# Expert weights mapped to partitions in contiguous runs: a two-block transformer kernel with two mixture-of-experts layers

## Chip, cores, metric

The kernel runs on one core of one Trainium2 chip, in one launch. The metric is the device time in microseconds. Everything is float32.

## What is computed

The reference runs 512 tokens of width 1024 through a first block (an even layer with pooling and differential attention, an odd layer with latent attention and a gated delta rule, each with a gated embedding layer behind it) and then, with 16 meta tokens put in front, through a second block of two layers: forgetting attention and a gated recurrence, each followed by a mixture of experts. The change touches the two mixtures alone:

```python
def hier_moe(h, w_grp, b_grp, w_rt, b_rt, w_up, w_down):     # h is already normalised
    # pick the best of 4 groups of experts, then the best 2 of its 8 experts
    ...
    def expert_block(args):
        xb, e = args                                        # 64 rows of tokens, one expert
        gate_up = xb @ w_up[e]                              # 1024 x 1024
        a, u = jnp.split(gate_up, 2, axis=-1)
        return (jax.nn.silu(a) * u) @ w_down[e]             # 512 x 1024
    ...
```

There are 32 experts a layer, so a layer reads 32 up matrices of 4096 KB and 32 down matrices of 2048 KB.

## The kernel before

The program is a list of stages, each a block in which the five engines run their own instruction lists; the next stage starts when all of them are through with the block. SBUF holds a ring of four weight buffers of 16 KB a partition, the transposed hidden rows `hT` (8 x 528 floats a partition), the rows themselves, and an arena that the stages share.

A mixture layer (`moe_layer`) has five stages. `stage_norm` squares and scales the rows, transposes them on TensorE (L365) and multiplies by the layer's gain on the way out of PSUM (VectorE, L343). In the same block SyncE issues what its argument `ahead` names: four small loads of the router (L2113 to L2116) and the weights of the first two experts (`first_pair`: up, down, up, down). `stage_route` waits for the router's loads (`loaded.at(64)`), computes logits with TensorE (L373, products of 36 columns) and picks experts in a long chain of VectorE steps. `stage_dispatch` scatters the rows of `keep`, which are normalised but not yet multiplied by the gain, into `x_rows` in HBM, 64 slots an expert. `stage_experts` is the loop. `stage_combine` gathers the results and adds them to the hidden rows.

`stage_experts` runs 16 times over a pair of experts. The up weights have two buffers, one over two ring buffers (`weight_ring` in the profile) and one in the arena; the down weights have the other two ring buffers. So each expert of a pair has its own buffers, and a buffer is loaded again as soon as the product that reads it is done (SyncE waits in the order up 0, down 0, up 1, down 1). In an iteration:

- SyncE loads 128 rows, those of both experts (L2364); TensorE transposes them in eight instructions (L2368), VectorE places them in `xT` with the gain (L2374).
- `tensor_up` (L2381): per expert 8 slices of the contraction times 2 halves of the columns, 512 columns each. The row block of 64 is the stationary operand, the weights are the moving one. The two halves q go to PSUM partitions 0 to 63 and 64 to 127. The profile shows each product as two instructions, 32 an expert.
- ScalarE takes silu of the first half (L2437), VectorE multiplies (L2455), TensorE transposes the hidden block (L2386), ScalarE places it (L2439).
- `tensor_down` (L2393): 16 instructions an expert. VectorE copies the result (L2459), ScalarE's queue stores it.

A weight matrix is mapped as `(k p)`: partition p holds the rows p, 128 + p, 256 + p and so on, each a run of 4 KB in HBM. Because the up products' columns are split in the order `(s q c)` (s: gate or value, q: half, c: 256 columns), a product reads runs of 256 neighbouring floats.

Of the kernel before, what the change touches and what calls it, by code (L numbers as in the profile page):

```python
# [13 lines left out]
P = 128  # L14
D = 1024
KD = D // P
# [21 lines left out]
ROWS = 64  # L38
# [37 lines left out]
class Signal:  # L76


    def __init__(self, sem):
        self.sem, self.base, self.count = sem, 0, 0  # L80
# [289 lines left out]
def products(nc, out, left, right):  # L370

    for i, (l, r) in enumerate(zip(left, right)):
        last = nc.tensor.matmul(out, l, r, start=i == 0, stop=i == len(left) - 1)  # L373
    return last
# [310 lines left out]
class Pooling:  # L685
# [11 lines left out]
    def load(self, sp):  # L697
        a = self.g.a
        sp.dma_start(self.scale, a["ev_pool_scale"].rearrange("a (n p) -> p (a n)", p=P), allow_slow_non_contiguous=True).then_inc(*self.loaded.up(16))
        sp.wait_ge(*self.zeroed.at(1))  # L700
        for n in range(2):
            for m in range(2):
                sp.dma_start(self.wp[64 * m:64 * m + 64, n, 64 * m:64 * m + 64], a["ev_pool_w"][2 * n + m]).then_inc(*self.loaded.up(16))
# [1375 lines left out]
class ExpertWeights:  # L2079
# [7 lines left out]
        self.wu, self.wd = g.a["moe_w_up_2"][layer], g.a["moe_w_down_2"][layer]  # L2087

    def load_up(self, sp, e, n):
        return sp.dma_start(self.up[n], self.wu[bass.ds(e, 1)].rearrange("a (k p) f -> p (a k) f", p=P))  # L2090

    def load_down(self, sp, e, n):
        return sp.dma_start(self.down[n], self.wd[bass.ds(e, 1)].rearrange("a (k p) f -> p (a k) f", p=P))

    def first_pair(self, sp):

# [5 lines left out]
class Router:  # L2102


    def __init__(self, g, layer):
        self.layer, self.a = layer, g.a
        self.w = g.take(KD, GROUPS + NEXP)
        self.bias = g.take(GROUPS + NEXP)
        self.loaded = g.sig("router_loaded")

    def load(self, sp):
        w, bias, a, n = self.w, self.bias, self.a, self.layer
        sp.dma_start(w[:, :, 0:GROUPS], a["moe_w_grp_2"][n].rearrange("(k p) n -> p k n", p=P), allow_slow_non_contiguous=True).then_inc(*self.loaded.up(16))  # L2113
        sp.dma_start(w[:, :, GROUPS:], a["moe_w_rt_2"][n].rearrange("(k p) n -> p k n", p=P)).then_inc(*self.loaded.up(16))
        sp.dma_start(bias[:, 0:GROUPS], a["moe_b_grp_2"][n:n + 1].to_broadcast([P, GROUPS])).then_inc(*self.loaded.up(16))
        sp.dma_start(bias[:, GROUPS:], a["moe_b_rt_2"][n:n + 1].to_broadcast([P, NEXP])).then_inc(*self.loaded.up(16))  # L2116


def moe_layer(g, layer, ring_upto):
    g.top = 0  # L2120
    keep = g.take(5, D)

    gw = g.take(2, 5)
    dest = g.take(2, 5).bitcast(I32)
    over = g.take(OVER + 1).bitcast(I32)
    g.top += (-g.top) % 8
    weights = ExpertWeights(g, layer)
    router = Router(g, layer)

    def ahead(sp):  # L2130
        router.load(sp)
        weights.first_pair(sp)

    tiles = XT if layer else ALLT
    stage_norm(g, tiles, g.gain(4 + layer), g.fed, keep, ahead)
    stage_route(g, tiles, router, gw, dest, over)
    stage_dispatch(g, tiles, keep, dest)
    stage_experts(g, layer, over, weights)
    g.top = 5 * D + 64
    stage_combine(g, tiles, gw, dest, ring_upto)  # L2140
    g.top = 0


def stage_route(g, tiles, router, gw, dest, over):

    nc = g.nc
    mark = g.top
    loaded = router.loaded
# [23 lines left out]
    with nc.Block() as block:  # L2172
        @block.tensor
        def _(pe):
            pe.wait_ge(*loaded.at(64))
            for i, t in enumerate(tiles):
                a, n = TILES[t]
                last = products(nc, g.psum[0:n, i, 0:NL], [g.hT[:, k, a:a + n] for k in range(KD)], [w[:, k, :] for k in range(KD)])
                last.then_inc(*ready.up())

            pe.wait_ge(*counted.at(1))
            for i, t in enumerate(tiles):
                n = TILES[t][1]
                left = [one[0:TILES[k][1], 0:n] for k in tiles if k < t] + [g.c("before")[0:n, 0:n]]
                products(nc, g.psum[0:n, 5, i * NEXP:(i + 1) * NEXP], left, [both[0:TILES[k][1], k, :] for k in tiles if k <= t])
            products(nc, g.psum[:, 6, 0:NEXP], [one[0:TILES[k][1], :] for k in tiles], [both[0:TILES[k][1], k, :] for k in tiles]).then_inc(*counts_ready.up())
# [9 lines left out]
        def _(dve):  # L2196
# [20 lines left out]
            dve.wait_ge(*chain.last())  # L2217
            v.memset(C, 0.0).then_inc(*chain.up())
            dve.wait_ge(*chain.last())
            dve.wait_ge(*loaded.at(64))  # L2220
            for i, t in enumerate(tiles):
                n = TILES[t][1]
                dve.wait_ge(*ready.at(i + 1))
# [50 lines left out]
            for i, t in enumerate(tiles):  # L2274
                n = TILES[t][1]
# [66 lines left out]
def stage_experts(g, layer, over, weights):  # L2342


    nc = g.nc
# [2 lines left out]
             "gated", "gate_silu", "hidden_transposed", "hidden_placed", "down_ready", "result_placed", "result_free_0", "result_free_1"]  # L2348
    x_in, x_turned, x_placed, up_ready, hid, silu, h_turned, h_placed, dn_ready, y_placed, y_free0, y_free1 = g.sig(*names)
    up_in, dn_in, y_free = weights.up_in, weights.down_in, (y_free0, y_free1)  # L2350
    gain = g.gain(4 + layer)
    up, down = weights.up, weights.down

    x = g.hT[:, 0:2, 0:512]
    xT = g.hT[:, 2:4, 0:512].rearrange("p a (k r) -> p a k r", k=4)
    s = g.hT[:, 6, 0:256]
    act_ = g.hT[:, 6, 256:512]
# [2 lines left out]
    xr, yr = g.a["x_rows"], g.a["y_rows"]  # L2360
    PAIRS = NEXP // 2

    def load_rows(sp, blk, rows):
        return sp.dma_start(x[0:rows, :, :], xr[bass.ds(blk * ROWS, rows)].rearrange("r (a c) -> r a c", a=2))  # L2364

    def tensor_rows():
        for c in range(KD):
            last = nc.tensor.transpose(g.psum[:, c // 4, (c % 4) * P:(c % 4 + 1) * P], x[:, c // 4, (c % 4) * P:(c % 4 + 1) * P], g.c("identity"))  # L2368
        return last

    def place_rows():
# [3 lines left out]
        return last  # L2375

    def tensor_up(n):
        wv = up[n].rearrange("p k (s q c) -> p k q s c", s=2, q=2)
        for k in range(KD):
            for q in range(2):  # L2380
                last = nc.tensor.matmul(g.psum[64 * q:64 * q + 64, 2 + n, :].rearrange("p (s c) -> p s c", s=2), xT[:, k // 4, k % 4, ROWS * n:ROWS * n + ROWS], wv[:, k, q, :, :], start=k == 0, stop=k == KD - 1)  # L2381
        return last

    def tensor_hidden():
# [17 lines left out]
    with nc.Block() as block:  # L2402
        @block.sync
        def _(sp):
            load_rows(sp, 0, P).then_inc(x_in.sem, 16)
            with sp.Fori(1, PAIRS) as i:
                sp.wait_ge(x_turned.sem, i + x_turned.base)
                load_rows(sp, 2 * i, P).then_inc(x_in.sem, 16)
                for n in range(2):

                    sp.wait_ge(up_ready.sem, 2 * i + (up_ready.base + n - 1))
                    weights.load_up(sp, 2 * i + n, n).then_inc(up_in[n].sem, 16)

                    sp.wait_ge(dn_ready.sem, 2 * i + (dn_ready.base + n - 1))
                    weights.load_down(sp, 2 * i + n, n).then_inc(dn_in[n].sem, 16)

        @block.tensor
        def _(pe):
            with pe.Fori(0, PAIRS) as i:
                pe.wait_ge(x_in.sem, 16 * i + (x_in.base + 16))  # L2420
                tensor_rows().then_inc(x_turned.sem, 1)
                pe.wait_ge(x_placed.sem, i + (x_placed.base + 1))
                for n in range(2):
                    pe.wait_ge(up_in[n].sem, 16 * i + (up_in[n].base + 16))
                    tensor_up(n).then_inc(up_ready.sem, 1)
                    pe.wait_ge(hid.sem, 2 * i + (hid.base + n + 1))
                    tensor_hidden().then_inc(h_turned.sem, 1)
                    pe.wait_ge(h_placed.sem, 2 * i + (h_placed.base + n + 1))
                    pe.wait_ge(dn_in[n].sem, 16 * i + (dn_in[n].base + 16))
                    tensor_down(n).then_inc(dn_ready.sem, 1)  # L2430
# [41 lines left out]
    with nc.Block() as block:  # L2472
# [8 lines left out]
        @block.sync  # L2481
        def _(sp):
            def body(j):
                e = sp.value_load(over[0:1, bass.ds(j, 1)], min_val=0, max_val=NEXP - 1)
                sp.wait_ge(done, j + 1)
                load_rows(sp, j + NEXP, ROWS).then_inc(rows_l, 16)
                weights.load_up(sp, e, 0).then_inc(up_l, 16)
                weights.load_down(sp, e, 0).then_inc(down_l, 16)
            each(sp, body)

        @block.tensor
        def _(pe):
            def body(j):
                pe.wait_ge(rows_l, 16 * j + 16)
                tensor_rows().then_inc(rT, 1)
                pe.wait_ge(rp, j + 1)
                pe.wait_ge(up_l, 16 * j + 16)
                tensor_up(0).then_inc(ur, 1)
                pe.wait_ge(ga, j + 1)
                tensor_hidden().then_inc(hT_, 1)  # L2500
                pe.wait_ge(hp, j + 1)
                pe.wait_ge(down_l, 16 * j + 16)
                tensor_down(0).then_inc(dr, 1)
            each(pe, body)
# [641 lines left out]
```

## Time and profile before

| | us |
|---|---|
| median of three runs | 3334.73 |
| lowest, highest | 3331.75, 3338.49 |
| the profiled execution: time | 3341.96 |
| the profiled execution: span | 3340.1 |
| PE busy, share of the span | 80% |
| DVE, ACT, POOL busy | 26%, 15%, 13% |
| mean granted TensorE clock | 0.874 |

Durations come from the profiled execution. Engines are PE (TensorE), PEld (its weight loads), DVE (VectorE), ACT (ScalarE), POOL (GpSimd) and SP (SyncE); SPq is SyncE's queue of issues. A row of a window has the window and its length, the busy time and number of instructions of PE, PEld, DVE, ACT and POOL, then the granted clock as a share of full speed, the mean busy share of the 16 DMA engines, and GB/s. `out<-in` names tensors of the program.

### The profile page before, as it was taken

The numbers are of one execution on the slowest core, as the hardware profiler recorded it, in microseconds if no ns is written. First come the engines' busy times: TensorE is split into PE (matmuls) and PEld (weight loads), VectorE is DVE, ScalarE is ACT, GpSimd is POOL, SyncE is SP. The second block draws the span as 40 slices with busy tenths as digits, with TensorE's granted clock in tenths as the row PEclk, the third lists the DMA queues.
The fourth block names the chain that finished last, engine by engine and source line by source line (L and its number), as shares of the span: only waits on it lengthen the run. The fifth ranks groups of instructions, "written<-read, shape, count | busy, mean of one in ns | idle before, by whom it ended". The sixth has DMA issues, their size and how long they took to land. (4 is left out here: it accounts for less than half of the span.)

```text
span 3340.1 us, 31732 instructions
## 1 busy us (share of the span) xinstructions
PE 2668.4 (80%) x12346; PEld 1339.6 (40%) x12346; DVE 871.8 (26%) x1847; ACT 498.9 (15%) x1154; POOL 448.6 (13%) x681
## 2 busy tenths in 40 slices
PE   6988888995757898999838777775989875777774
PEld 3654444452556544456432222222435442222221
DVE  2315411124366213205131110103055422101111
ACT  1102101012300002115100000001134300000000
POOL 1510001006010002217110000002044200000001
PEclk9995599997778999989959999997989887998987
DMA  4220012102000004203349999995101035999997
GB/s 148 76 91 1 0 54 76 51 16 91 1 1 1 26 8 147 76 8 120 143 195 367 416 415 417 415 416 172 36 27 52 26 153 220 415 417 415 416 415 289
DMA packets 196225, 570.13 MB, mean 171 GB/s; under 512 B 21040, under 2 KB 31152, under 8 KB 195984
## 3 DMA queue, kind: packets, MB, share of 16 engines
q1 hardware_dynamic: 181136, 534.77, 41.0%
q0 software_dynamic: 4736, 17.04, 1.4%
q10 hardware_dynamic: 10240, 16.79, 1.4%
q8 instruction: 74, 1.21, 0.1%
q14 instruction: 39, 0.32, 0.0%
HBM read 524.23 MB, written 44.21 MB: 170 GB/s over the span
## 5 line engine op out<-in xcount | busy, mean ns | idle before, releaser
L373 PE MATMUL psum<-weight_ring,hidden_T 128*128 128x512 f32 (+3 forms) x1792 | 714.1, 557 | 14.5 <-DMA arena<-in_p_T 10.4
L373 PEld LDWEIGHTS psum<-weight_ring,hidden_T 128*128 128x128 f32 x1792 | 339.0, 194 | 364.8 <-issue 290.6
L2381 PE MATMUL psum<-weight_ring,hidden_T 128*64 128x512 f32 x1024 | 284.0, 717 | 102.8 <-DMA weight_ring<-in_moe_w_up 95.9
L2393 PE MATMUL psum<-weight_ring,hidden_T 128*64 128x512 f32 x1024 | 233.8, 599 | 30.3 <-ACT hidden_T L2439 30.3
L2381 PE MATMUL psum<-arena,hidden_T 128*64 128x512 f32 x1024 | 230.0, 602 | 27.1 <-DMA arena<-in_moe_w_up 27.0
L2381 PEld LDWEIGHTS psum<-weight_ring,hidden_T 128*64 128x64 f32 x1024 | 94.5, 164 | 272.0 <-issue 257.1
L2455 DVE TENSOR_TENSOR hidden_T<-hidden_T,psum 128x256 f32<-128x256 f32 x64 | 27.0, 422 | 603.4 <-ACT hidden_T L2437 603.4
L2563 POOL DMA_INDIRECT arena<-expert_rows_out,arena x18 | 21.3, 1185 | 1067.8 <-PEq L2552 1062.9
L275 POOL TENSOR_SCALAR arena<-arena 128x1 f32<-128x1 f32 (+5 forms) x97 | 20.9, 215 | 941.5 <-ACT arena L1091 186.6
L2381 PEld LDWEIGHTS psum<-arena,hidden_T 128*64 128x64 f32 x1024 | 71.8, 138 | 184.6 <-issue 132.8
L2393 PEld LDWEIGHTS psum<-weight_ring,hidden_T 128*64 128x64 f32 x1024 | 67.8, 136 | 155.1 <-issue 109.6
L2437 ACT ACTIVATE hidden_T<-psum 128x256 f32<-128x256 f32 x64 | 24.5, 383 | 692.9 <-PE psum L2381 692.9
L2685 PE MATMUL psum<-weight_ring,hidden_T 128*128 128x512 f32 x256 | 123.4, 612 | 0.0
L2459 DVE COPY arena<-psum 128x512 f32<-128x512 f32 x64 | 44.3, 692 | 301.7 <-PE psum L2393 301.7
L373 PE MATMUL psum<-hidden_T,weight_ring 128*128 128x512 f32 (+2 forms) x288 | 119.4, 576 | 3.5 <-PEq L298 3.5
L373 PE MATMUL psum<-weight_ring,arena 128*128 128x512 f32 (+1 forms) x240 | 115.8, 629 | 2.1 <-PEq L2662 1.0
L2677 PE MATMUL psum<-hidden_T,weight_ring 128*128 128x512 f32 x256 | 111.4, 595 | 3.8 <-PEq L298 1.8
L365 PE MATMUL psum<-constants,arena 128*128 128x128 f32 (+1 forms) x216 | 40.2, 363 | 82.2 <-ACT arena L325 80.7
L279 POOL TENSOR_TENSOR arena<-arena,constants 128x1 f32<-128x1 f32 (+5 forms) x89 | 94.9, 1066 | 7.4
L2368 PE MATMUL psum<-constants,hidden_T 128*128 128x128 f32 x256 | 36.7, 289 | 65.0 <-DMA hidden_T<-expert_rows_in 65.0
L373 PE MATMUL psum<-arena,hidden_T 128*128 128x36 f32 (+2 forms) x264 | 61.8, 413 | 30.9 <-PEq L298 18.3
L457 DVE TENSOR_TENSOR hidden<-hidden,psum 128x512 f32<-128x512 f32 (+1 forms) x34 | 23.4, 687 | 221.4 <-PE psum L373 220.8
(461 smaller groups left out, 3169.9 us busy)
## 6 DMA issues: line engine op xcount, KB each, us to landing
weight_ring<-in_moe_w_up SPq DMA_DIRECT2D x32, 4096.0 KB, 23.3
weight_ring<-in_moe_w_down SPq DMA_DIRECT2D x64, 2048.0 KB, 24.0
arena<-in_moe_w_up SPq DMA_DIRECT2D x32, 4096.0 KB, 25.5
hidden_T<-expert_rows_in SPq DMA_DIRECT2D x32, 512.0 KB, 19.9
expert_rows_out<-arena ACTq DMA_DIRECT2D x128, 128.0 KB, 5.5
weight_ring<-in_hg_w_in SPq DMA_DIRECT2D x8, 2048.0 KB, 8.8
weight_ring<-in_ev_w_in SPq DMA_DIRECT2D x8, 1536.0 KB, 6.7
weight_ring<-in_fox_w_in SPq DMA_DIRECT2D x6, 2048.0 KB, 8.5
```

Source lines behind the costliest of these rows:

```text
L279: g.nc.gpsimd.tensor_tensor(out, out, power, ALU.pow).then_inc(*done.up())
L365: last = nc.tensor.transpose(g.psum[:, 2 * (i % 2) + c // 4, (c % 4) * P:(c % 4) * P + n], src, g.c("identity")[0:n, 0:n])
L373: last = nc.tensor.matmul(out, l, r, start=i == 0, stop=i == len(left) - 1)
L457: nc.vector.tensor_tensor(dst, dst, g.psum[0:n, u % 4, :], ALU.add).then_inc(*added.up())
L2368: last = nc.tensor.transpose(g.psum[:, c // 4, (c % 4) * P:(c % 4 + 1) * P], x[:, c // 4, (c % 4) * P:(c % 4 + 1) * P], g.c("identity"))
L2381: last = nc.tensor.matmul(g.psum[64 * q:64 * q + 64, 2 + n, :].rearrange("p (s c) -> p s c", s=2), xT[:, k // 4, k % 4, ROWS * n:ROWS * n ...
L2393: last = nc.tensor.matmul(g.psum[64 * q:64 * q + 64, 6 + n, :], aT[:, k % 2, 64 * (k // 2):64 * (k // 2) + 64], down[n][:, k, 512 * q:512 ...
L2437: nc.scalar.activation(s, g.psum[:, 2 + n, 0:256], ACT.Silu).then_inc(silu.sem, 1)
L2455: nc.vector.tensor_tensor(act_, s, g.psum[:, 2 + n, 256:512], ALU.mult).then_inc(hid.sem, 1)
L2459: nc.vector.tensor_copy(y[n], g.psum[:, 6 + n, :]).then_inc(y_placed.sem, 1)
L2677: last = mm(bank(u % 2), w[:, k, (x % 4) * P:(x % 4 + 1) * P], g.hT[:, k, META:], **flags)
L2685: last = mm(bank(u % 2), g.hT[:, k, a:a + n], w[:, k, :], **flags)
```

## The change

The weights are mapped as `(p k)`: partition p holds eight neighbouring rows of the up matrix, 8p to 8p + 7, and four neighbouring rows of the down matrix, 4p to 4p + 3. Slice k of the contraction is then every eighth channel, so the row transposes take every eighth element of a row (`x[:, c::KD]`), and the gain that is multiplied in behind them must be laid out likewise. That layout, `row_gain`, comes from eight more small loads in the router's list (each 16 partitions of 8 single floats), and the router's waits count them (192 instead of 64). The rows of tokens now lie in one run of 1024 floats instead of two of 512. Hidden channel 4p + k must stand in slice k of the down product, so the up product takes its columns at a step of four: `(s c q j)` instead of `(s q c)`.

```diff
     def load_up(self, sp, e, n):
-        return sp.dma_start(self.up[n], self.wu[bass.ds(e, 1)].rearrange("a (k p) f -> p (a k) f", p=P))
+        return sp.dma_start(self.up[n], self.wu[bass.ds(e, 1)].rearrange("a (p k) f -> p (a k) f", p=P))
     def load_down(self, sp, e, n):
-        return sp.dma_start(self.down[n], self.wd[bass.ds(e, 1)].rearrange("a (k p) f -> p (a k) f", p=P))
+        return sp.dma_start(self.down[n], self.wd[bass.ds(e, 1)].rearrange("a (p k) f -> p (a k) f", p=P))
...
+        g.row_gain = g.take(KD)
...
+        by_chunk = a["norm_gains"].rearrange("(r k) (n q) -> n q r k", k=KD, q=KD)
+        for q in range(KD):
+            sp.dma_start(self.g.row_gain[16 * q:16 * q + 16, :], by_chunk[4 + n, q], allow_slow_non_contiguous=True).then_inc(*self.loaded.up(16))
...
-            pe.wait_ge(*loaded.at(64))
+            pe.wait_ge(*loaded.at(192))
...
-            dve.wait_ge(*loaded.at(64))
+            dve.wait_ge(*loaded.at(192))
...
-    gain = g.gain(4 + layer)
+    gain = g.row_gain
...
-    x = g.hT[:, 0:2, 0:512]
+    x = g.hT.rearrange("p k n -> p (k n)")[:, 0:D]
...
-        return sp.dma_start(x[0:rows, :, :], xr[bass.ds(blk * ROWS, rows)].rearrange("r (a c) -> r a c", a=2))
+        return sp.dma_start(x[0:rows, :], xr[bass.ds(blk * ROWS, rows)])
...
-            last = nc.tensor.transpose(g.psum[:, c // 4, (c % 4) * P:(c % 4 + 1) * P], x[:, c // 4, (c % 4) * P:(c % 4 + 1) * P], g.c("identity"))
+            last = nc.tensor.transpose(g.psum[:, c // 4, (c % 4) * P:(c % 4 + 1) * P], x[:, c::KD], g.c("identity"))
...
-        wv = up[n].rearrange("p k (s q c) -> p k q s c", s=2, q=2)
+        wv = up[n].rearrange("p k (s c q j) -> p k q s j c", s=2, q=2, j=2)
         for k in range(KD):
             for q in range(2):
-                last = nc.tensor.matmul(g.psum[64 * q:64 * q + 64, 2 + n, :].rearrange("p (s c) -> p s c", s=2), xT[:, k // 4, k % 4, ROWS * n:ROWS * n + ROWS], wv[:, k, q, :, :], start=k == 0, stop=k == KD - 1)
+                last = nc.tensor.matmul(g.psum[64 * q:64 * q + 64, 2 + n, :].rearrange("p (s j c) -> p s j c", s=2, j=2), xT[:, k // 4, k % 4, ROWS * n:ROWS * n + ROWS], wv[:, k, q, :, :, :], start=k == 0, stop=k == KD - 1)
```

## Rows read from the trace of the kernel before

**Rows 1.** The page's slices: GB/s of the DMA engines in 40 slices.
```profile
GB/s 148 76 91 1 0 54 76 51 16 91 1 1 1 26 8 147 76 8 120 143 195 367 416 415 417 415 416 172 36 27 52 26 153 220 415 417 415 416 415 289
```
**Rows 2.** Window over the first expert stage; the DMA queues in 1850 to 2200 us.
```profile
1748.26:2262.60 514.34, 404.86 (x1728) 137.63 (x1728) 55.56 (x95) 43.77 (x79) 0.00 (x0) 0.93 0.99 398
...
DMA packets 39795, 145.50 MB, mean 416 GB/s; under 512 B 1522, under 2 KB 1522, under 8 KB 39795
```
**Rows 3.** The page's groups of the up product: busy, mean ns, idle before.
```profile
L2381 PE MATMUL psum<-weight_ring,hidden_T 128*64 128x512 f32 x1024 | 284.0, 717 | 102.8 <-DMA weight_ring<-in_moe_w_up 95.9
L2381 PE MATMUL psum<-arena,hidden_T 128*64 128x512 f32 x1024 | 230.0, 602 | 27.1 <-DMA arena<-in_moe_w_up 27.0
```
**Rows 4.** Timeline of TensorE, second expert pair: start us, us, what.
```profile
1778.78 1.10 PE L2368 MATMUL psum<-constants,hidden_T 128*128 128x128 f32 x8
1781.26 7.09 PE L2381 MATMUL psum<-weight_ring,hidden_T 128*64 128x512 f32 x32 [1.38 <-DVE hidden_T L2374]
...
1793.67 7.04 PE L2381 MATMUL psum<-arena,hidden_T 128*64 128x512 f32 x32
...
1806.15 1.09 PE L2368 MATMUL psum<-constants,hidden_T 128*128 128x128 f32 x8
```
**Rows 5.** Timeline: first transposes and last copy of each expert stage.
```profile
1748.26 1.97 PE L2368 MATMUL psum<-constants,hidden_T 128*128 128x128 f32 x8 [33.63 <-DMA hidden_T<-expert_rows_in]
...
2262.66 0.69 DVE L2459 COPY arena<-psum 128x512 f32<-128x512 f32 x1 [4.67 <-PE psum L2393]
...
2791.68 1.97 PE L2368 MATMUL psum<-constants,hidden_T 128*128 128x128 f32 x8 [31.41 <-DMA hidden_T<-expert_rows_in]
...
3307.16 0.69 DVE L2459 COPY arena<-psum 128x512 f32<-128x512 f32 x1 [4.67 <-PE psum L2393]
```
**Rows 6.** VectorE groups by form: reductions, contiguous (L2298, L910), strided (L2238, L2976).
```profile
L2298 DVE TENSOR_REDUCE arena<-arena 128x5 f32<-128x160 f32 x6 | 1.9, 321 | 0.2
L2238 DVE TENSOR_REDUCE arena<-arena 128x40 f32<-128x160 f32 x1 | 0.4, 420 | 0.0
...
L910 DVE TENSOR_REDUCE arena<-arena 128x6 f32<-128x768 f32 x4 | 3.8, 953 | 0.1
...
L2976 DVE TENSOR_REDUCE weight_ring<-weight_ring 128x128 f32<-128x768 f32 x8 | 12.1, 1510 | 0.3
```
**Rows 7.** TensorE groups by form: four 32-column products side by side.
```profile
L389 PE MATMUL psum<-weight_ring,arena 128*32 128x128 f32 x512 | 16.2, 274 | 1.6 <-POOL arena L439 1.6
```
**Rows 8.** Timeline from the norm to the router, both layers; windows (columns of rows 2).
```profile
1664.71 15.58 SPq L2093 DMA_DIRECT2D weight_ring<-in_moe_w_down  x1
...
1671.12 2.48 DVE L343 TENSOR_TENSOR hidden_T<-psum,norm_gains 128x512 f32<-128x512 f32 x4 [0.36 <-PE psum L365]
1680.73 11.51 PE L373 MATMUL psum<-arena,hidden_T 128*16 128x36 f32 x64 [8.76 <-PEq L298]
...
2731.02 13.84 PE L373 MATMUL psum<-arena,hidden_T 128*128 128x36 f32 x64 [9.56 <-PEq L298]
...
1690.00:1695.00 5.00, 5.00 (x25) 5.00 (x25) 0.20 (x1) 0.00 (x0) 0.00 (x0) 0.50 1.03 423
...
1700.00:1705.00 5.00, 0.13 (x2) 0.12 (x2) 4.28 (x24) 0.21 (x1) 0.00 (x0) 0.50 0.00 0
```
**Rows 9.** Packets and issues of the page; issue and landing of two small loads.
```profile
DMA packets 196225, 570.13 MB, mean 171 GB/s; under 512 B 21040, under 2 KB 31152, under 8 KB 195984
...
q8 instruction: 74, 1.21, 0.1%
q14 instruction: 39, 0.32, 0.0%
...
1.23 0.49 SPq L212 DMA_DIRECT2D constants<-in_constants  x1
...
constants<-in_constants SPq DMA_DIRECT2D x1, 1664.5 KB, 6.8
...
arena<-in_moe_w_grp SPq DMA_DIRECT2D x2, 16.0 KB, 2.3
```

More of the change, by code:

```diff
@@ L2105, in __init__ @@
     def __init__(self, g, layer):
-        self.layer, self.a = layer, g.a
+        self.g, self.layer, self.a = g, layer, g.a
         self.w = g.take(KD, GROUPS + NEXP)
         self.bias = g.take(GROUPS + NEXP)
+        g.row_gain = g.take(KD)
         self.loaded = g.sig("router_loaded")
```

## The prediction

> **What bounds the kernel now.** I read the page first, by its slices of DMA throughput [rows 1]. Twice it stands at 413 to 418 GB/s for many slices in a row: these are the two expert stages, the only place where the changed loads run. The window over the first of them [rows 2] says the same in one number each: 514 us, DMA share 0.99, TensorE busy 405 us. In the steady part the queues move 416 GB/s with 4 KB packets, and the packets' own time fills the 16 engines. The groups of the up product [rows 3] show whom TensorE waits for there: of the idle time before them, 95.9 and 27.0 us end with the landing of an up matrix. So the transfers bound these stages. How near TensorE is behind them is to be read where they do not yet bind: the first expert pairs of a stage find their weights loaded. The second pair of the first stage [rows 4] runs from its row transposes at 1778.78 to the next pair's at 1806.15: 27.37 us, with no wait for a transfer. The stage from its first transpose to its last copy [rows 5] takes 2263.35 - 1748.26 = 515.1 us, and 516.2 us in the second layer: some 32.2 us a pair. TensorE and its chain have 4.8 us of slack in a pair, no more. 14.1 us of the 27.37 are the up products, 7.09 and 7.04 us an expert.
>
> **Part 1, the up product's reads.** Its instructions keep count and shape (32 an expert, 512 columns), but the moving operand now takes every fourth float32 of the weight row, so neighbours stand 16 bytes apart instead of 4. Each now lasts some 600 ns [rows 3], yet 32 of them take 7.04 us [rows 4]: they run two at a time, one for each half of the up columns, and a pair follows the last after (7.04 - 0.60) / 15 = 430 ns, 0.84 ns a column for each of the two streams. No row shows TensorE reading at a stride. The nearest rows are VectorE's [rows 6]. A reduction of 160 contiguous elements takes 321 ns, one of 768 takes 953: 1.04 ns an element and 155 ns fixed. The same 160 elements read 32 bytes apart take 420 ns, so (420 - 155) / 160 = 1.66 ns an element; 768 read 512 bytes apart take 1510 ns, 1.76 ns an element. An SBUF read in which each element stands apart from the last costs 1.66 to 1.76 ns on that engine, and TensorE asks for one every 0.84 ns. Lower end: nothing, if TensorE's port brings separate elements at that pace. For that speaks [rows 7]: four 32-column products side by side read four streams of float32, 512 instructions in 16.2 us, 126 ns for four times 128 columns, so the engine is fed by more than one stream at near full pace; but all of them contiguous. Upper end: 1.76 ns an element, or, if both streams of a pair share it, 3.3 to 3.5. I take 1.66 ns a column with the streams independent, since the stride of 32 bytes is the nearest one measured and [rows 7] shows that streams do not add up. A pair of instructions then takes 512 x 1.66 = 850 ns instead of 430: 420 ns more, 16 times an expert, 6.7 us an expert, 13.4 us an expert pair.
>
> Weighed against the notes: the Trainium skill, "Advanced Engine Details and Errata", section "SBUF Cachelines", says that reads want at least two hits in a 16-byte line, and that a new line for each access is penalised. With float32 sixteen bytes apart there is one hit. VectorE's two strided rows agree (1.66 and 1.76 ns against 1.04); no row here tries it on TensorE. The page gives no factor; by it the sum is that of my forecast in kind, and without it that of the first rival.
>
> **Part 2, the row transposes.** Eight an expert pair; the stationary operand takes every eighth float32 of the row. They take 1.10 us now, 137 ns each. At 1.66 ns an element a load of 128 takes 212 ns: 75 ns more, 0.6 us a pair. Lower end nothing. They lie on TensorE's chain.
>
> **Part 3, does it show?** The 4.8 us of slack a pair are used up when the up products grow by more than a third. With 13.4 + 0.6 us more they are, and then the chain runs at its own pace. That pace for a whole stage: first pair 30.52 us (1748.26 to 1778.78, with a slow clock at its start), 15 more at 27.37: 441 us. Add 16 x 14.0 = 224: 665 us. Against 515.1 and 516.2 us that is 150 and 149 more, together +299 us. The granted clock is 0.93 over the stages now; with no transfer to wait for it stays up, as in the pair of [rows 4], which is the one that I count with. Nothing takes the extra time back: the next layer needs the sums of all experts.
>
> **Part 4, the transfers.** Each partition of an up matrix now reads one run of 32 KB instead of eight rows of 4 KB, a down matrix 16 KB instead of four; the rows of tokens go as 4 KB instead of twice 2 KB. Bytes are the same. That a run goes as one packet can be counted [rows 9]: of 196225 packets 195984 are under 8 KB, so 241 are above; 74 + 39 are instruction fetches, and the 128 left are the 128 partitions of the constants (1664.5 KB, 13 KB each). Throughput can hardly rise, the engines being filled: between 416 GB/s as now and 423, the best 5 us with 4 KB packets [rows 8], 1.7%, up to 8.5 us a stage. In my forecast the transfers no longer bind, so it counts nothing. By the Trainium skill, "DMA: Bandwidth & Descriptors", section "Why small descriptors are slow (HBM only)", each packet has some 3 bus cycles of its own, 2.3% of one of 4 KB; that estimate would give 11 us a stage in place of 8.5 and leaves the forecast as it is.
>
> **Part 5, SyncE's queue before the router.** This gives something back. SyncE issues the first pair's four loads in the norm block, and its last issue takes 15.58 us, to 1680.29, since descriptors back up [rows 8]. The norm's last VectorE step is done at 1673.60, yet the router's products start at 1680.73, 0.44 us after SyncE: TensorE idles 8.76 us there, 9.56 us in the second layer. With 128 runs a load instead of 1024 and 512 the issues should take what the constants took, about 0.5 us each. The eight new gain loads (128 runs of 4 bytes each) stand ahead of them: 8 x 0.49 = 3.9 us of issue, and the wait counts them too. The router's group weights, 1024 short runs, land in 2.3 us [rows 9], so the gains are there by about 1669, SyncE is through by 1668.2, and the router starts at 1673.60 + 0.44: 6.7 us earlier, and 0.8 more in the second layer, where the idle time is that much longer: -14.2 us in all. The first pair's own landing moves 3.9 us later, to about 1700 (DMA is idle from 1700 now), while the first token rows are transposed at 1748 [rows 5]: hidden. If the issues still back up, the 3.9 us come on top in each layer: +7.8. The row gain takes eight columns of the arena; the multiplication by it is as before. VectorE and ScalarE have the same work.
>
> **Sum.** +299 - 14 = +285 us on the profiled execution's own time of 3341.96 (span 3340.1): 3627. The median of the runs, 3334.73, is 7.2 us lower than that execution; so 3620 us.
>
> **Rivals.** (Each as a median, 7.2 us below the sum.)
> (a) TensorE reads at this stride at full pace, or less than a third slower: the slack hides it. Then the transfers still bind, and what is left is part 5 and up to 17 us of part 4: 3341.96 - 14.2 - 8.5 - 7.2 = 3312 (3303 to 3320): faster. For it speak [rows 7] and that the port is another than VectorE's. Against it VectorE's rows. It decides at 27.37 + 4.8 us a pair: a pitch of 430 + 4800 / 32 = 580 ns a pair of instructions.
> (b) As (a), but the issues still back up: +7.8 us, less what throughput gives: 3326 to 3342, about no change.
> (c) The stride costs a factor and not a time: 1.66 / 1.04 = 1.6 times. 686 ns a pair, 8.2 us an expert pair more, 441 + 131 = 572 us a stage: +114 - 14 = +100: 3435.
> (d) Both streams share the line rate: pitch 1700 ns, 40.6 us an expert pair more: 441 + 650 = 1091 us a stage, about 4470.
> (e) Long runs slow the transfers, since each engine then stays long in one place of the memory and stores wait behind long packets. No row speaks for it; the constants' 13 KB packets ran at the common rate. At 5% it is +50 us: 3370 with the rest of (a).
>
> **How the numbers follow.** Forecast (with its upper end of 1.76 ns, no part 2 at the lower) 0.50; (c) and what lies between 0.07; (d) 0.03; (e) 0.02; (a) 0.31; (b) 0.07. The likeliest case's own range: 3600 (part 2 free) to 3700: 512 x 1.76 = 901 ns, 15.1 us a pair, 441 + 242 + 10 = 693 us a stage, +355, and +7.8 if issues back up, less 7.2. The range for 8 in 10 reaches down to (a): 3303 to 3700. By signs (a measurement of this kernel tells about 0.2%, 6.7 us, from no change): faster 0.31, same 0.07, slower 0.62.
>
> **What the profile after would show.** The up product's 32 instructions in 13.6 us instead of 7.04; GB/s in the stages falling to some 320 (416 x 515 / 665); idle before L2381 no longer ended by a transfer; granted clock in the stages near 1. Packets in all from 196225 to some 110000 (64 x 1408 fewer and the rows'). Router's products right after the norm, SyncE's issues at 0.5 us. The forecast is wrong if the up products keep 7 us: then the stages stay at 515 us and only the router's start moves.

## The result, and the profile after

The changed kernel takes 3700.39 us in the median of four runs (3698.12 to 3701.68); the kernel before took 3336.61 beside it. The ratio is 1.1077, with a 95% interval of 1.1054 to 1.1100: 364 us slower. The prediction was 3620 us, with a range of 3600 to 3700 for the likeliest case; direction and mechanism were as forecast, the size 80 us short, and the median 0.4 us past that range's upper end.

The page of the profiled execution (time 3699.86, span 3698.1), its slices of throughput, packets, the up product (L2385, before L2381) and the down product (L2397, before L2393):

```profile
GB/s 151 75 60 0 23 26 92 37 82 1 1 1 30 92 86 30 30 188 197 295 304 314 312 320 311 313 181 46 24 48 24 182 237 323 326 306 299 312 314 176
...
DMA packets 112513, 570.14 MB, mean 154 GB/s; under 512 B 23344, under 2 KB 33456, under 8 KB 95888
...
L2385 PE MATMUL psum<-weight_ring,hidden_T 128*64 128x512 f32 x1024 | 468.8, 1083 | 44.2 <-DVE hidden_T L2378 44.2
L2385 PE MATMUL psum<-arena,hidden_T 128*64 128x512 f32 x1024 | 466.7, 1078 | 0.0
...
L2397 PE MATMUL psum<-weight_ring,hidden_T 128*64 128x512 f32 x1024 | 271.9, 680 | 30.3 <-ACT hidden_T L2443 30.3
```

The flat 416 GB/s of [rows 1] is gone: the stages stand at 295 to 326. The up product is busy 935.5 us in place of 514.0 [rows 3], and no idle time before it ends with a transfer any more: the 44.2 us before it all end with VectorE's placing of the transposed rows (L2378). The bound has passed from the transfers to TensorE, though the bytes are the same and lie in fewer packets. The down product, which the change does not touch, is busy 38.1 us longer too; the group of before has 233.8 us, mean 599 ns.

The timeline of TensorE over a pair with its weights in place, and a later expert, against [rows 4]:

```profile
1790.35 1.16 PE L2372 MATMUL psum<-constants,hidden_T 128*128 128x128 f32 x8
1792.89 14.61 PE L2385 MATMUL psum<-weight_ring,hidden_T 128*64 128x512 f32 x32 [1.38 <-DVE hidden_T L2378]
...
1809.34 3.65 PE L2397 MATMUL psum<-weight_ring,hidden_T 128*64 128x512 f32 x16 [0.47 <-ACT hidden_T L2443]
1812.83 14.57 PE L2385 MATMUL psum<-arena,hidden_T 128*64 128x512 f32 x32
...
1832.83 1.16 PE L2372 MATMUL psum<-constants,hidden_T 128*128 128x128 f32 x8
...
2397.03 5.35 PE L2397 MATMUL psum<-weight_ring,hidden_T 128*64 128x512 f32 x16 [0.47 <-ACT hidden_T L2443]
```

The pair takes 42.48 us instead of 27.37, and 15.05 of the 15.11 more are the up products: 7.52 and 7.53 us an expert. The weight loads inside one of them give the pitch:

```profile
1796.51 0.16 PEld L2385 LDWEIGHTS psum<-weight_ring,hidden_T 128*64 128x64 f32 x2 [0.74 <-issue]
1797.41 0.16 PEld L2385 LDWEIGHTS psum<-weight_ring,hidden_T 128*64 128x64 f32 x2 [0.74 <-issue]
```

A pair of instructions now follows the last after 0.90 us, not 0.43: 1.76 ns a column for each of the two streams.

First transposes and last copy of both stages, against [rows 5]:

```profile
1746.87 1.97 PE L2372 MATMUL psum<-constants,hidden_T 128*128 128x128 f32 x8 [33.22 <-DMA hidden_T<-expert_rows_in]
...
2446.58 0.69 DVE L2463 COPY arena<-psum 128x512 f32<-128x512 f32 x1 [4.67 <-PE psum L2397]
...
2964.01 1.97 PE L2372 MATMUL psum<-constants,hidden_T 128*128 128x128 f32 x8 [30.86 <-DMA hidden_T<-expert_rows_in]
...
3665.50 0.69 DVE L2463 COPY arena<-psum 128x512 f32<-128x512 f32 x1 [6.22 <-PE psum L2397]
```

The stages take 700.4 and 702.2 us, 185.3 and 186.0 more than before: +371.3. Around the router of the first layer, against [rows 8]:

```profile
1668.39 5.17 SPq L2120 DMA_DIRECT2D arena<-in_norm_gains  x8
...
1675.18 0.53 SPq L2093 DMA_DIRECT2D weight_ring<-in_moe_w_down  x1
...
1677.17 2.48 DVE L343 TENSOR_TENSOR hidden_T<-psum,norm_gains 128x512 f32<-128x512 f32 x4 [0.28 <-PE psum L365]
1679.97 14.70 PE L373 MATMUL psum<-arena,hidden_T 128*16 128x36 f32 x80 [1.87 <-PEq L298]
```

SyncE's last issue is through before the norm is. From SyncE's first issue in the block (1666.23, before 1660.09) to the router it is 13.74 us, before 20.64: 6.9 us less. In the second layer it is 2906.36 - 2894.27 = 12.09 against 2731.02 - 2711.05 = 19.97: 7.9 less. 371.3 - 14.8 = 356.5 is the whole difference of the spans, 358.0, but for 1.5 us. These 1.5 us are a net: SyncE's first issue in the block comes 6.1 us later than before, after code that the change does not touch, and the stretches between these stages give 4.6 us back. Differences of a few microseconds between two profiled executions mean no more than that.

### The profile page after: what moved, and what is told of

It is laid out like the page before. It is cut to its first block and busy times, and to the rows that moved or that the text cites. A ratio compares the mean times of both kernels' runs of the same rounds, so it can differ in the third digit from the quotient of the medians.

```text
span 3698.1 us, 31748 instructions
## 1 busy us (share of the span) xinstructions
PE 3128.2 (85%) x12346; PEld 1349.4 (36%) x12346; DVE 872.3 (24%) x1847; ACT 498.8 (13%) x1154; POOL 447.3 (12%) x681
## 2 busy tenths in 40 slices
DMA packets 112513, 570.14 MB, mean 154 GB/s; under 512 B 23344, under 2 KB 33456, under 8 KB 95888
## 5 line engine op out<-in xcount | busy, mean ns | idle before, releaser
L2385 PE MATMUL psum<-weight_ring,hidden_T 128*64 128x512 f32 x1024 | 468.8, 1083 | 44.2 <-DVE hidden_T L2378 44.2
L2385 PE MATMUL psum<-arena,hidden_T 128*64 128x512 f32 x1024 | 466.7, 1078 | 0.0
L2397 PE MATMUL psum<-weight_ring,hidden_T 128*64 128x512 f32 x1024 | 271.9, 680 | 30.3 <-ACT hidden_T L2443 30.3
L2385 PEld LDWEIGHTS psum<-weight_ring,hidden_T 128*64 128x64 f32 x1024 | 80.9, 155 | 380.1 <-issue 329.4
L2385 PEld LDWEIGHTS psum<-arena,hidden_T 128*64 128x64 f32 x1024 | 81.7, 152 | 349.5 <-issue 349.5
L2397 PEld LDWEIGHTS psum<-weight_ring,hidden_T 128*64 128x64 f32 x1024 | 76.8, 154 | 184.3 <-issue 138.7
L2463 DVE COPY arena<-psum 128x512 f32<-128x512 f32 x64 | 44.2, 691 | 339.9 <-PE psum L2397 339.9
L2372 PE MATMUL psum<-constants,hidden_T 128*128 128x128 f32 x256 | 38.7, 296 | 64.1 <-DMA hidden_T<-expert_rows_in 64.1
L2390 PE MATMUL psum<-constants,hidden_T 128*128 128x128 f32 x128 | 28.0, 300 | 60.0 <-DVE hidden_T L2459 60.0
```

What stands on the lines that cost most here:

```text
L2390: last = nc.tensor.transpose(g.psum[:, 4, j * P:(j + 1) * P], act_[:, j * P:(j + 1) * P], g.c("identity"))
L2397: last = nc.tensor.matmul(g.psum[64 * q:64 * q + 64, 6 + n, :], aT[:, k % 2, 64 * (k // 2):64 * (k // 2) + 64], down[n][:, k, 512 * q:512 ...
L2463: nc.vector.tensor_copy(y[n], g.psum[:, 6 + n, :]).then_inc(y_placed.sem, 1)
```

## Experiments

**Whose loss is it, and what is left without it.** The changed kernel with the columns of the up product in runs again:

```diff
-        wv = up[n].rearrange("p k (s c q j) -> p k q s j c", s=2, q=2, j=2)
+        wv = up[n].rearrange("p k (s q c) -> p k q s c", s=2, q=2)
```

> The changed kernel with its up columns read in the old order (runs of 256 neighbouring floats); long runs in memory, strided row transposes and gain loads stay. It leaves out that hidden channels arrive in the order of the down matrix's rows, so what it computes differs. Theory A (the read 16 bytes apart is the whole cost): 32 up instructions take 7.04 us again, the stages are bound by transfers again at about 515 us, and the time is that of before less the router's earlier start and up to 17 us of throughput: 3300 to 3325 us. Rival B (the long runs or the strided transposes cost): it stays above 3400 us.

One run: 3290.03 us, beside 3349.62 for the kernel before. Its page, and its DMA queues in 1850 to 2200 us:

```profile
L2385 PE MATMUL psum<-weight_ring,hidden_T 128*64 128x512 f32 x1024 | 254.0, 653 | 70.5 <-DMA weight_ring<-in_moe_w_up 51.1
L2385 PE MATMUL psum<-arena,hidden_T 128*64 128x512 f32 x1024 | 239.7, 623 | 43.9 <-DMA arena<-in_moe_w_up 43.9
...
DMA packets 11649, 150.53 MB, mean 430 GB/s; under 512 B 1616, under 2 KB 1616, under 8 KB 6011
```

This kernel computes something else, and ran once, as did the halves in turn, the half strided and the other steps below. All the rest of the change is in it, strided row transposes and gain loads too, and it is faster than before. The step of the up columns is the loss, and it covers a gain: the transfers bind again, and run at 430 GB/s where they ran at 416 [rows 2].

The other way round, the kernel before with only the down matrices in runs and the step in the up product that this needs:

```diff
     def load_down(self, sp, e, n):
-        ... self.wd[bass.ds(e, 1)].rearrange("a (k p) f -> p (a k) f", p=P))
+        ... self.wd[bass.ds(e, 1)].rearrange("a (p k) f -> p (a k) f", p=P))
...
-        wv = up[n].rearrange("p k (s q c) -> p k q s c", s=2, q=2)
+        wv = up[n].rearrange("p k (s c q j) -> p k q s j c", s=2, q=2, j=2)
```

> The kernel before with the down matrices alone in runs of 16 KB and the up product's columns at a step of four; up matrices, row transposes, token rows and gains as before. Theory: the up product's reads are the whole loss, so this kernel has it in full: 32 of its instructions in 14.6 us, each stage some 185 us longer; less the router's start if short runs of the two up loads no longer back up (0 to -14), no gain loads: 3695 to 3712 us, ratio about 1.11. Rival: part of the loss of 364 us belongs to the row transposes, the gain and the rows' layout; then it is below 3680.

3695.92 us, ratio 1.1058 (1.1020 to 1.1095), span 3691.5. Stages of 688.7 and 691.4 us. The long issue stays in front of the router:

```profile
1667.17 15.57 SPq L2093 DMA_DIRECT2D weight_ring<-in_moe_w_down  x1
1683.18 14.92 PE L373 MATMUL psum<-arena,hidden_T 128*16 128x36 f32 x80 [8.57 <-PEq L298]
...
L2393 PE MATMUL psum<-weight_ring,hidden_T 128*64 128x512 f32 x1024 | 248.9, 631 | 30.2 <-ACT hidden_T L2439 30.2
```

The step alone gives the whole loss: 351.4 us of span. Its four runs lie between 3679.57 and 3710.52 us, so by time alone it can't be told from the full change. The full change has 14.8 us less at the routers and 23.0 us more in the down product (271.9 against 248.9 us), which gives 351.4 - 14.8 + 23.0 = 359.6 against the 358.0 measured, both from one profiled execution each.

**One stream or two.** Two theories gave the same 0.90 us: each stream is limited by itself, or the two of a pair share something that strided reads fill. First the halves one after the other (the loops over `k` and `q` change places), so that only one stream runs. The sums are the same:

> The changed kernel with its up product's two column halves one after the other (q outside k) instead of alternating, so that no two strided streams run side by side; the same sums. Theory A1 (each stream by itself gets one element per 1.78 ns): an instruction alone takes 912 ns, 32 take 29 us instead of 14.6, 14.6 us more an expert, 467 a stage: about 4630 us. Theory A2 (the two streams share a supply of one separate element per 0.89 ns): alone each runs at 456 ns, 32 take 14.6 us, and the time stays at about 3700 us.

4381.43 us. The weight loads show the pitch, and the seam between the halves:

```profile
1864.67 0.16 PEld L2385 LDWEIGHTS psum<-weight_ring,hidden_T 128*64 128x64 f32 x1 [0.74 <-issue]
1865.57 0.19 PEld L2385 LDWEIGHTS psum<-weight_ring,hidden_T 128*64 128x64 f32 x3 [0.74 <-issue]
1866.47 0.17 PEld L2385 LDWEIGHTS psum<-weight_ring,hidden_T 128*64 128x64 f32 x2 [0.71 <-issue]
1867.37 0.17 PEld L2385 LDWEIGHTS psum<-weight_ring,hidden_T 128*64 128x64 f32 x2 [0.73 <-issue]
1868.29 0.16 PEld L2385 LDWEIGHTS psum<-weight_ring,hidden_T 128*64 128x64 f32 x1 [0.75 <-issue]
```

One instruction alone takes the 0.90 us that two side by side take. So the two streams share nothing that limits them here: the limit is in each stream. I expected 29 us an expert and it is 25.4, since four instructions at the seam run beside those of the other half (the rows x3, x2 and x2): 28 times 0.90 us.

Then one half strided and the other in runs:

```diff
+        wc = up[n].rearrange("p k (s q j c) -> p k q s j c", s=2, q=2, j=2)
...
-                last = nc.tensor.matmul(..., wv[:, k, q, :, :, :], ...)
+                last = nc.tensor.matmul(..., (wv if q else wc)[:, k, q, :, :, :], ...)
```

> The changed kernel with half q = 0 of the up product read in contiguous runs and half q = 1 at the step of four; some columns are computed twice and others not at all, so what it computes differs. A1 (each stream limited by itself): a pair lasts as long as its strided one, 912 ns, 32 instructions 14.6 us, time about 3700 us. A2 (shared supply of 0.89 ns per separate 16 bytes): 1 + 1/4 fetches a column, 1.11 ns, 570 ns a pair, 32 take 9.2 us, about 3380 to 3400 us. If streams merely averaged: 671 ns, 10.8 us.

3736.71 us.

```profile
1856.78 14.67 PE L2386 MATMUL psum<-arena,hidden_T 128*64 128x512 f32 x32
```

14.67 us for the 32 instructions, mean of one 852 and 845 ns (the mean of a quick and a slow one), weight loads 0.90 us apart. A pair lasts as long as its strided one. The 37 us above the changed kernel hardly come from the up product: the down product is busy 307.8 us here, 35.9 more than the 271.9 of the changed kernel, and the up product only 5.3 more.

Two other causes can be set aside. In all these versions the products write PSUM in runs of neighbouring floats, as before; only the reads change. And transfers into SBUF do not set the pace: the last strided product of the changed kernel's first stage, from 2426.29 us, takes 14.73 us, while the DMA engines stand at a share of 0.08 and 19 GB/s (window 2426.29 to 2440.00).

**Distance between the elements.** A step of two floats (8 bytes) and of eight (32 bytes), one kernel for each `+` line:

```diff
-        wv = up[n].rearrange("p k (s c q j) -> p k q s j c", s=2, q=2, j=2)
+        wv = up[n].rearrange("p k (s c q) -> p k q s c", s=2, q=2)            # step 2
+        wv = up[n].rearrange("p k (s c q j) -> p k q s j c", s=2, q=2, j=4)   # step 8
```

> The changed kernel with the up columns read at a step of two floats (8 bytes) instead of four; hidden channels reach the down product in another order, so what it computes differs. If the limit is on 16-byte pieces, each serves two elements here: A1 gives full pace (7.04 us for 32 instructions), A2 gives 456 ns a pair (7.3 us); both about 3310 us. If any step other than one costs a fetch for each element, 14.6 us and 3700 us.

> The changed kernel with the up columns read at a step of eight floats (32 bytes); hidden channels reach the down product in another order, so what it computes differs. If what counts is one 16-byte piece for each element, 32 instructions take 14.6 us as at a step of four, and the time is 3700 us. If the cost grows with the distance, more: 29 us and 4600.

3292.12 and 3687.77 us. A product of an expert at full clock, step 2 and below it step 8:

```profile
1778.86 7.42 PE L2385 MATMUL psum<-weight_ring,hidden_T 128*64 128x512 f32 x32 [1.38 <-DVE hidden_T L2378]
```

```profile
1786.29 14.90 PE L2385 MATMUL psum<-weight_ring,hidden_T 128*64 128x512 f32 x32 [1.38 <-DVE hidden_T L2378]
```

By the starts of the weight loads, the pair's pitch is 0.43 us at 4 bytes, 0.45 at 8, 0.90 at 16 and 0.92 at 32. It is a step and not a slope: two floats of one 16-byte piece keep nearly full pace, one float of each piece costs double, and farther apart adds 2%. That is what the Trainium skill, "Advanced Engine Details and Errata", section "SBUF Cachelines", says in kind (16-byte lines, at least two hits wanted in each); the factor of 2.1 and that TensorE's moving operand falls under it are from these runs.

**The gain loads and SyncE's issues.** The kernel before with the eight gain loads and the router's waits on 192, all else as it was (the multiplication keeps the old gain):

> The kernel before with the eight gain loads added and waited for, and never used otherwise. If the issues behind them still back up, as the prediction has it for short runs: SyncE ends its block 3.9 to 5.2 us later in each layer, and the router with it: +8 to +10 us, ratio 1.002 to 1.003. Rival: the queue holds a fixed number of bytes or descriptors and the start of the transfers only moves: the same number. If the loads were free: 1.000.

3348.65 us, ratio 1.0029 (1.0009 to 1.0050), 8.5 us slower.

```profile
1660.69 5.16 SPq L2120 DMA_DIRECT2D arena<-in_norm_gains  x8
...
1667.70 14.54 SPq L2093 DMA_DIRECT2D weight_ring<-in_moe_w_down  x1
...
1682.68 7.67 PE L373 MATMUL psum<-arena,hidden_T 128*16 128x36 f32 x46 [12.28 <-PEq L298]
```

With short runs behind them the new loads push the long issue back, and the router starts 24.16 us after SyncE's first issue (1658.52) instead of 20.64; in the second layer it is 22.57 instead of 19.97. That is 6.1 us in the trace, and the ratio gives 3 to 17. In the changed kernel the same eight loads are covered: no short runs back up behind them, so SyncE is through at 1675.71, 9.5 us after its first issue, and the norm only at 1679.65.

The kernel before with the first pair's four loads issued in the router's block:

```diff
     def ahead(sp):
         router.load(sp)
-        weights.first_pair(sp)
...
+        @block.sync                    # in stage_route
+        def _(sp):
+            weights.first_pair(sp)
```

> The kernel before, but the four weight loads of the first expert pair are issued by SyncE in the router's block instead of the norm's; mapping, router loads and products as before. The two versions with long runs and contiguous columns gained 37 to 45 us. Theory (two sources): some 14 us of it come from the router's start, which no longer waits for SyncE's backed-up issue; this kernel shows that part alone: router's products 6.7 us after the block's start earlier in layer one and about 7.5 in layer two, 3326 us, ratio 0.996; the long issue of about 15 us stands then in the router's block, where VectorE's chain hides it. The rest, some 25 to 30 us, is transfer throughput (416 to 430 GB/s). Rival (one source): the router's start is worth nothing in the end because something else of the same block is late next, and all of the gain is throughput: 3340 us, ratio 1.000.

3327.31 us, ratio 0.9935 (0.9909 to 0.9961).

```profile
1679.48 14.40 PE L373 MATMUL psum<-arena,hidden_T 128*16 128x36 f32 x80 [1.83 <-PEq L298]
...
1682.20 12.60 SPq L2093 DMA_DIRECT2D weight_ring<-in_moe_w_down  x1
```

The router starts 13.89 and 12.09 us after SyncE's first issue in the norm's block, before 20.64 and 19.97: 14.6 us in both layers, which lies within the 13 to 30 us that the ratio gives. The last two issues still take 14.3 and 13.8 us together in the two layers (16.9 and 16.3 before), and cost nothing where they stand now. The queue was worth what the prediction said.

**Can the gain be had without the loss?** The changed kernel with only the up matrices in long runs, down matrices as before, so that no step is needed in the up product:

```diff
     def load_down(self, sp, e, n):
-        ... self.wd[bass.ds(e, 1)].rearrange("a (p k) f -> p (a k) f", p=P))
+        ... self.wd[bass.ds(e, 1)].rearrange("a (k p) f -> p (a k) f", p=P))
...
-        wv = up[n].rearrange("p k (s c q j) -> p k q s j c", s=2, q=2, j=2)
+        wv = up[n].rearrange("p k (s q c) -> p k q s c", s=2, q=2)
```

> Only the up matrices in long runs (32 KB a partition), down matrices mapped as before, so the up columns need no step and the result is the reference's. Theory A (the read 16 bytes apart was the whole cost): up products 7.04 us an expert, stages bound by transfers; a third of the weight bytes stays in 4 KB packets, so throughput between 416 and the 430 GB/s that all long runs gave: about 425; 3295 to 3310 us, ratio about 0.99. Rival B (mapping the up matrix itself costs): 3400 us or more.

3303.19 us, ratio 0.9888 (0.9865 to 0.9911), with 425 GB/s in 1850 to 2200 us. Then all of the long runs, with up columns in runs of 256 and the step of four moved from the 512-column moving operand to the small transposes of the hidden block (eight products of 64 x 64 with the identity, their stationary operand strided):

```diff
-        for j in range(2):
-            last = nc.tensor.transpose(g.psum[:, 4, j * P:(j + 1) * P], act_[:, j * P:(j + 1) * P], g.c("identity"))
+        for k in range(4):
+            for q in range(2):
+                r = slice(64 * q, 64 * q + 64)
+                last = nc.tensor.matmul(g.psum[r, 4, 64 * k:64 * k + 64], act_[:, k::4], g.c("identity")[:, r], start=True, stop=True)
...
-                last = nc.tensor.matmul(..., aT[:, k % 2, 64 * (k // 2):64 * (k // 2) + 64], ...)
+                last = nc.tensor.matmul(..., aT[:, k // 2, 64 * (k % 2):64 * (k % 2) + 64], ...)
```

> All matrices in long runs, up columns in runs of 256; the step of four is moved into the transposes of the hidden block (eight products with the identity of 64 x 64, whose stationary operand takes every fourth of 256 columns, in place of two transposes of 128 x 128). The result is the reference's. If only moving operands pay and stationary ones hardly: about 0.5 us more an expert on TensorE's chain, hidden behind the transfers, throughput 430 GB/s: 3285 to 3300 us, ratio 0.985. If stationary reads at a step cost as much as moving ones, 16 loads x 64 x 1.8 ns = 1.8 us an expert, 30.5 us a pair against 31.1 us of transfers: still near 3300.

3298.28 us, ratio 0.9866 (0.9843 to 0.9889): 45 us faster than before by the ratio (42 by the medians), and the fastest that has the reference's sums, though its interval overlaps with that of the last. Its timeline, and its queues in 1850 to 2200 us:

```profile
2102.76 1.17 PE L2392 MATMUL psum<-constants,hidden_T 128*64 128x64 f32 x16 [0.94 <-DVE hidden_T L2461]
2104.42 3.65 PE L2399 MATMUL psum<-weight_ring,hidden_T 128*64 128x512 f32 x16 [0.48 <-ACT hidden_T L2445]
...
2111.29 8.78 PE L2385 MATMUL psum<-weight_ring,hidden_T 128*64 128x512 f32 x32 [2.13 <-DMA weight_ring<-in_moe_w_up]
2121.01 1.17 PE L2392 MATMUL psum<-constants,hidden_T 128*64 128x64 f32 x16 [0.93 <-DVE hidden_T L2461]
2122.66 5.35 PE L2399 MATMUL psum<-weight_ring,hidden_T 128*64 128x512 f32 x16 [0.48 <-ACT hidden_T L2445]
...
DMA packets 11614, 150.67 MB, mean 430 GB/s; under 512 B 1616, under 2 KB 1616, under 8 KB 5968
```

Moving the step costs 0.7 us an expert here (1.17 us for the sixteen small instructions, 0.44 for the two contiguous ones), against 7.5 us in the up product, and the slack of the pair takes nearly all of it: the stages last 502.0 and 500.1 us, 5.3 us more in sum than with contiguous columns and no step anywhere (498.2 and 498.6). Against the kernel before they are 29.2 us shorter in sum, and the routers start 14.7 us earlier. These 43.9 us are near the 45 of the ratio. The profiled execution is 54.0 us shorter in span, 5.5 of which it gained before the first router, where the change has done nothing yet.

## Why the prediction was right in kind and 80 us short

- **What bounds, and the slack.** Right. The slack of 4.8 us a pair was used up, and nothing took the time back.
- **Part 1, the up product.** Mechanism right, and so is that the streams are independent. The term "I take 1.66 ns a column" was too small: 1.76 ns was measured, 0.90 us a pair of instructions and not 0.85. I took VectorE's row for 32 bytes as the nearer one; TensorE, with 1.76 ns at 16 bytes and 1.80 at 32, behaves as VectorE at 512 (1.76 in [rows 6]). 15.05 us an expert pair, not 13.4.
- **Part 2, row transposes.** "A load of 128 takes 212 ns: 75 ns more" was close for the load, which went from 141 to 193 ns (medians of the line). But a load runs beside the product before it, and eight transposes took 1.16 us instead of 1.10: 0.06 us a pair, not 0.6. Its lower end, nothing, was the right value.
- **Part 3, the stage.** Predicted 665 us, measured 700.4. The first pair took 43.48 us, predicted 30.52 + 14.0: -1.0. The other fifteen at full clock would take 42.48 each, predicted 41.37: +16.7, the pitch less the transposes. They took 656.9 us in all, 43.79 each: another +19.7. This last term is the step "with no transfer to wait for it stays up", and it failed. The windows (columns of [rows 2]) over a strided product, over the strided product ahead of the slow down product above, over that down product, and over the whole stage:

```profile
1792.90:1807.50 14.60, 14.60 (x32) 2.52 (x32) 0.00 (x0) 1.18 (x1) 0.00 (x0) 1.00 0.69 294
...
2381.00:2395.00 14.00, 14.00 (x32) 2.29 (x28) 0.61 (x1) 0.00 (x0) 0.00 (x0) 1.00 0.77 328
2397.00:2402.40 5.40, 5.37 (x17) 1.56 (x18) 0.00 (x0) 0.00 (x0) 0.00 (x0) 0.68 0.92 394
1746.87:2447.27 700.40, 632.41 (x1728) 141.96 (x1728) 56.21 (x96) 43.77 (x79) 0.00 (x0) 0.96 0.71 292
```

  TensorE had been busy for the whole product before, yet the clock is at its lower level for part of the down product. Eleven of the stage's 32 down products took 5.16 to 5.35 us instead of 3.65, 18.1 us more in sum; in the second stage it was twelve of 32. In the kernel before all 64 took 3.65.
- **Part 4, the transfers.** In the changed kernel they don't bind, so the term is rightly nothing. "Throughput can hardly rise", at most to 423 GB/s, was wrong: 425 with long up runs, 430 with both. A busy share of 0.99 did not mean that no faster pace was possible: with fewer packets the engines, just as busy, moved more. By the Trainium skill, "DMA: Bandwidth & Descriptors", section "Why small descriptors are slow (HBM only)", each packet costs some 3 cycles of its own beside one for every 32 bytes; my estimate from that is 2.3% of a packet of 4 KB and 0.3% of one of 32 KB, so a gain of 2.0%, and 3.4% was measured. The direction agrees, and what the rest is stays open.
- **Part 5, SyncE's queue.** Right: -6.9 and -7.9 us, predicted -6.7 and -7.5. The gain loads took 5.17 us, not 3.9 (0.65 each), and still stood clear of the path.
- **The sum.** Predicted +299 - 14; measured +371.3 - 14.8. That, with the 1.5 us above, makes the profiled execution 72.9 us longer than its forecast of 3627 us. The other 7.5 us are the step from that execution to the median: 7.2 us were subtracted for it, but the changed kernel's four runs lie within 3.6 us. That the range's upper end fits so closely is partly luck. It took the right pitch of 1.76 ns, but also issues that still back up, which they did not; with the earlier routers it would be about 3675. The down product's 38.1 us, which no term had, filled the place, less some 17 us that part 2 had too much.
- **The rivals.** (a) decided at a pitch of 0.58 us; it was 0.90. Had I weighed it with 430 GB/s it would have stood near 3286 (3.4% of 1031 us are 35, not 8.5), and the kernel with contiguous columns took 3290. (b) did not happen; its price is shown by the gain loads alone: +8.5 us by the medians, predicted +7.8. (c) falls, with a factor of 2.1 at 16 bytes and 1.05 at 8. (d) is refuted by the halves in turn. (e) falls: long runs were faster, not slower.
- **What the profile would show.** No transfer before L2385 and the router's start as said. Throughput is near it, 295 to 326 GB/s for "some 320". Packets are 112513 for "some 110000", though "64 x 1408 fewer" is miscounted: the 1024 + 512 of an expert become 128 + 128, so 1280 fewer. The product took 14.6 us in place of 13.6, and the clock was 0.96 and not near 1.

## What to carry to other kernels

A layout that pleases the DMA engines is paid for where the data are read: if it puts the float32 of a wide moving operand 16 bytes or more apart, each of its columns costs double. Keep at least two of the floats that are read within each 16-byte piece (every second float cost 5%), or put the step where few elements pass (a small transpose, a stationary operand whose load runs beside a product). And before a change to transfers, work out how far behind them the next engine is: here it was 4.8 us in 32, and the change asked for 15.

## What the runs showed of the hardware

- A float32 moving operand: 0.43 us for 512 columns at a step of 4 bytes, 0.45 at 8, 0.90 at 16, 0.92 at 32; the same with one stream as with two side by side.
- The granted clock fell to its lower level in down products that follow a strided up product, or sixteen small transposes, with TensorE idle for hardly a microsecond between; the same short gaps stand before the 64 down products of the kernel before, and it fell in none of them. The down products were longer than before's by 38.1 us in the changed kernel, 15.1 with the step alone or with a step of eight, 52.5 with the halves in turn, 74.0 with one half strided, 40.6 with the step in the hidden transposes, and not at all with contiguous columns or a step of two. What in the work before sets it off was not tried.
- With the engines' share at 1.03 and 1.01 (1850 to 2200 us), weights moved at 416 GB/s in 4 KB packets and at 430 in packets of 16 and 32 KB; two experiments that left the packets at 4 KB kept 416.
- SyncE's last two of the four weight issues take 13.5 to 16.9 us together as long as up matrices go in 4 KB runs, wherever the issues stand (the kernel before, and three of the experiments); with long up runs they take about 1.
